# Where the expert-row pieces stand between the steps of two attention units, and two gate scalings one step earlier

## The chip, the cores and the metric

The kernel runs on one NeuronCore of a Trainium2 chip. TensorE (PE) multiplies matrices into PSUM, VectorE (DVE) and ScalarE (ACT) do the elementwise work, GpSimd (POOL) issues the indirect loads of expert rows, SyncE (SP) issues the weight loads. Each engine works through its own instructions in program order and waits on semaphores. The metric is the device time of one execution in microseconds (us); here the median of three executions.

## The reference

Two networks run one after the other on 256 tokens of width 1024, all in fp32. The first has two layers of attention, each followed by an expert layer:

```python
x = x + merged @ w_out[layer]
x = x + peer_ffn(rms_norm(x, norm2_g[layer]), w_query[layer], ...)
# peer_ffn, per token: 8 heads x 16 experts chosen by two top-k stages
act = gelu(einsum('td,ted->te', tb, expert_u[eb]))
out = einsum('te,ted->td', gb * act, expert_v[eb])
```

The second network, also of two layers, puts 16 meta tokens in front. A layer has a softmax mixer of 4 heads (MLA), a retention mixer of 4 heads with a gate `rg` that passes through silu, an output projection, and a gated FFN of width 2816.

## The kernel before

**First network.** Its 256 tokens make four expert units (2 token tiles x 2 layers, numbered 0 to 3). An expert unit has 128 rows per token. Row number n of all tokens is one indirect load (`row<-in_experts,idx`): 128 partitions x 2048 fp32, the u half and the v half of the chosen expert. DVE multiplies the u half with the token and sums it (line 1972, a *dot*), ACT applies gelu to four dots at once (line 1464), and the v half is added to `acc` with its weight (line 1955, an *acc*).

**Second network.** It has four units too (`layer2(v)`): units 0 and 1 are the two layers for meta tokens plus the first 128 tokens (144 columns), units 2 and 3 the same for the last 128 tokens. The body of each engine's `layer2` is a generator. The code between two `yield`s is a *step*; PE, ACT and DVE have the same 42 steps. On DVE: steps 0 to 5 norm, query and key parts; 6 and 7 rotate `rq`; 8 and 9 scale the keys and rotate `rk`; 10 to 15 softmax, value and decay work, head by head; 16 to 18 the output norms, which end with `yT` (lines 2282, 2291, 2293); 19 and 20 the residual add; 21 and 22 the second norm; 23 to 41 the FFN.

**What runs side by side.** Units 0 and 1 of the second network run together with the rows of expert unit 3. `last_order()` writes one list for all engines: a step of the unit, or one *piece* of row work (`"rows"`). There are 248 pieces (31 groups of 8). `SHARE2[s]` says how many of them, in proportion, stand in front of step s. A group of four rows is eight pieces on DVE:

- pieces 1 and 2 of a group: a dot of this group and an acc of the group before
- pieces 3 and 4: a dot each
- pieces 5 and 6: an acc each (in piece 5 of every eighth group also the gates of the next part)
- piece 7: the four weights (line 1989), after ACT's gelu
- piece 8: nothing, or in four of eight groups a part of the choice of the next experts: `best_keys`, `best_pairs`, `best_experts` twice

In this part PE has no work for the rows. ACT does the gelu in piece 5, once DVE has done the dot of piece 4; its other work waits behind it. POOL loads a row into the place of one ten rows earlier, when the acc of that one is done, so the order of the pieces on DVE also sets when row loads start. SP loads weight tiles of 2 MB into two places; the load of tile n+2 starts when PE has finished the last matmul of tile n (`layer2_taken`).

**The gate scaling.** `gate_scaled(p)` (line 2161) waits until PE has filled `rgA` or `rgB` and multiplies it with the norm factor. PE makes `rgA` at the end of its step 11 and `rgB` at the end of its step 13 (line 956, after the matmuls of `turn`, `values` and `ret_sums`). ACT takes the result through tanh (line 1522, `silu_gate(0)` in step 12, `silu_gate(1)` in step 14), and DVE finishes it in `gated` (line 2166, steps 12 and 14).

Of the kernel before, what the change touches and what calls it, by code (L numbers as in the profile page):

```python
# [241 lines left out]
def first_columns(b, start, stop, n):  # L242
# [2 lines left out]


TURN = 8
SHARE2 = ([0.6, 1.8, 0.8, 0.8, 0.9, 0.4, 0.9, 0.6, 0.8, 1.2, 1.6, 1.6, 1.6, 1.8, 1.6, 1.0, 2.0, 1.0, 1.0, 2.2, 1.6, 2.4, 0.0]
          + [1.4] + [2.1] * (FC // 2 - 1) + [1.4] * KC)
STEPS2 = len(SHARE2)  # L250


def last_order():

    beside = [0] * STEPS2 + [1] * (STEPS2 - KC)
    share = SHARE2 + SHARE2[:STEPS2 - KC]
    pieces = (PAIRS * GROUPS - 1) * TURN
# [16 lines left out]
def program(nc, x_in, meta_in, ws, c1_in, c2_in, fin_g, rel, k1_in, k2_in, euv, out):  # L274
    with ExitStack() as ctx:
# [1402 lines left out]
        def _(dve):  # L1678
# [331 lines left out]
            def layer2(v):  # L2010
# [10 lines left out]
                def bstep(ins):  # L2021
                    ins.then_inc(b_step, 1)
                    settled["b"] += 1

                def bsettle():
                    dve.wait_ge(b_step, settled["b"])
# [55 lines left out]
                def centered(name, dst, m, k):  # L2082
                    U.filled(dve, name)
                    b = U.bank(name)[0:m, :].rearrange("p (h e) -> p h e", h=RH)
                    bstep(dve.tensor_reduce(stb[0:m, 130:134], b, AX.X, ALU.add))
                    bsettle()
                    square = stb[0:m, 170 + k - 1:171 + k - 1]
                    bstep(dve.tensor_scalar(stb[0:m, 134:138], stb[0:m, 130:134], square, -1.0 / P, ALU.mult, ALU.mult))
                    bsettle()
                    U.inc(stt(dst.rearrange("p (h e) -> p h e", h=RH), b, square,  # L2090
                              stb[0:m, 134:138].unsqueeze(2).to_broadcast([m, RH, P]), ALU.mult, ALU.add), "b_rv")

                def s_read(name):
                    i = U.s_use(name)
                    U.wait(dve, "b_s", i + 1)
                    return S[(BASE["b_s"][v] + i) % 2]
# [20 lines left out]
                def decayed(h):  # L2117
                    b = s_read(f"r{h}")
                    if h >= 2:
                        U.wait(dve, "b_o", O_USES.index(f"r{h - 2}") + 1)  # L2120
                    d = k2st[:, K2_D + T2 * h:K2_D + T2 * (h + 1)]
                    if t:
                        tt_(rp[0:META, h % 2, 0:P], b[0:META, 0:P], d[0:META, T0:T2], ALU.mult)
                        m = tt_(rp[:, h % 2, P:3 * P], b[:, P:3 * P], d[:, 0:2 * P], ALU.mult)
                    else:
                        tt_(rp[0:META, h % 2, 0:T0], b[0:META, 0:T0], d[0:META, 0:T0], ALU.mult)
                        m = tt_(rp[:, h % 2, T0:T0 + P], b[:, T0:T0 + P], d[:, 0:P], ALU.mult)
                    U.inc(m, "b_sr")
# [28 lines left out]
                def gate_scaled(p):  # L2157
                    name = f"rg{'AB'[p]}"
                    U.filled(dve, name)
                    U.wait(dve, "b_rr", 4)  # L2160
                    U.inc(tt_((rot1 if t else rot0)[:, :, 0:T], two(U.bank(name)), each(bcs[:, 0:T], 2), ALU.mult), "b_rg")
# [95 lines left out]
                probs(1)  # L2257
                if not t:
                    centered("rvm", rvm[l][:], META, 2)
                yield  # L2260
                gate_scaled(0)
                logits(3)
                probs(2)
                decayed(0)
# [1 line left out]
                yield  # L2266
                probs(3)
                decayed(1)
                yield
                gate_scaled(1)  # L2270
                decayed(2)
                gated(1)
                yield
# [86 lines left out]
            for _ in window_order(1, attend, experts, layer2):  # L2360
                pass
# [174 lines left out]
```

## Time and profile before

| | |
|---|---|
| median of three executions | 2486.65 us (2485.22 to 2486.80) |
| the profiled execution, its own time | 2485.22 us |
| its span, first to last instruction | 2483.4 us |
| busy: PE, DVE, POOL, ACT | 2165.2, 1576.9, 632.3, 457.4 us |
| mean granted TensorE clock | 0.935 |
| mean DMA rate | 363 GB/s |

Busy shares are means over stages that differ. The stages of interest lie between 1419 and 2058 us: unit 0 up to the FFN (1419 to 1548), FFN of unit 0 (to 1752), unit 1 up to its FFN (to 1869), FFN of unit 1 (to 2058). In a line of the timeline the number in brackets is the idle time of the engine just ahead and what ended it; "issue" there means that the profile shows no releaser.

### The profile page before, as it was taken

To read this page: it belongs to the slowest core of one execution; us is meant where nothing else is said; L and a number is where in the kernel's file an instruction comes from. 1 tells how busy PE (TensorE), PEld (TensorE's weight loads), DVE (VectorE), ACT (ScalarE), POOL (GpSimd) and SP (SyncE) were. 2 spreads that over 40 slices of the span, in tenths; PEclk is the share of its full clock that TensorE was granted. 3 is DMA by queue.
4 is the path that set the end of the run, shared out by engine and by line. 5 is a ranking of instruction groups with operands and counts; after the bars stand their busy time and mean duration, and the time that the engine had idled before them with its cause. 6 is when DMAs were issued, how large, how long until landed. Compare 5 with 4: busy or idle time off the path is not lost.

```text
span 2483.4 us, 40088 instructions
## 1 busy us (share of the span) xinstructions
PE 2165.2 (87%) x16356; PEld 2006.1 (81%) x16356; DVE 1576.9 (63%) x4201; ACT 457.4 (18%) x984; POOL 632.3 (25%) x518
## 2 busy tenths in 40 slices
PE   9998899777889978688986788887887799999999
PEld 7887689777779868677986776877867798899799
DVE  1258688686777868869777689885788533312310
ACT  2210232101123011113301132100231012101100
POOL 0023334333334333334333223332133200000000
PEclk9999899989989979899998898989989899999999
DMA  8589999999999999999999977999979969468474
GB/s 330 186 372 422 421 421 418 422 421 419 422 414 417 422 411 421 418 423 411 392 421 418 420 310 312 415 422 403 371 293 403 423 227 387 174 242 314 167 256 154
DMA packets 106917, 900.95 MB, mean 363 GB/s; under 512 B 12748, under 2 KB 16880, under 8 KB 17904
## 3 DMA queue, kind: packets, MB, share of 16 engines
q0 software_dynamic: 73904, 537.43, 52.9%
q1 hardware_dynamic: 31728, 357.95, 36.4%
q8 instruction: 130, 2.13, 0.3%
q10 hardware_dynamic: 1104, 3.02, 0.3%
q14 instruction: 51, 0.42, 0.0%
HBM read 897.30 MB, written 1.05 MB: 362 GB/s over the span
## 4 chain that ended last, share of the span: by engine, by line
PE 39%; DMA 36%; DVE 18%; issue 4%; POOL 2%; ACT 1%; SPq 0%; DVEq 0%; POOLq 0%; ACTq 0%
DMA row<-in_experts,idx 20%; PE ea L956 11%; PE pa L956 10%; DMA more<-in_experts,idx 8%; DMA wring<-in_weights 8%; DVE row L1972 5%; DVE acc L1955 3%; PE ea L874 2%; PE pa L676 2%; PE pa L782 2%; POOL row L2388 1%; DVE topi L1864 1%; PE pa L829 1%; PE ea L964 1%; DVE topv L1860 1%
## 5 line engine op out<-in xcount | busy, mean ns | idle before, releaser
L2388 POOL DMA_INDIRECT row<-in_experts,idx x448 | 556.8, 1243 | 1198.7 <-DVE acc L1955 559.1
L1972 DVE CUSTOM_DVE_ANT_0 row<-row,h2n 128x1024 f32<-128x1024 f32 x448 | 534.9, 1221 | 187.4 <-DMA row<-in_experts,idx 186.5
L874 PE MATMUL ea<-diag,row 128*128 128x128 f32 x3808 | 497.7, 296 | 139.1 <-DVE diag L1994 139.1
L874 PEld LDWEIGHTS ea<-diag,row 128*128 128x128 f32 x3808 | 486.3, 211 | 152.1 <-DVE diag L1994 150.6
L1955 DVE SCALAR_TENSOR_TENSOR acc<-row,wgt,acc 128x1024 f32<-128x1024 f32 x207 | 265.1, 1281 | 2.0
L1464 ACT ACTIVATE gl<-dots 128x4 f32<-128x4 f32 x128 | 26.3, 206 | 945.1 <-DVE dots L1972 945.0
L956 PE MATMUL ea<-hB,wring 128*128 128x144 f32 (+1 forms) x1056 | 147.7, 304 | 20.9 <-DMA wring<-in_weights 20.9
L956 PEld LDWEIGHTS ea<-hB,wring 128*128 128x128 f32 x1056 | 144.0, 208 | 23.3 <-DMA wring<-in_weights 22.8
L956 PE MATMUL pa<-hB,wring 128*128 128x144 f32 (+1 forms) x1056 | 137.6, 291 | 17.6 <-DMA wring<-in_weights 15.0
L956 PEld LDWEIGHTS pa<-hB,wring 128*128 128x128 f32 x1056 | 133.9, 197 | 21.0 <-DMA wring<-in_weights 16.2
L782 PE MATMUL pa<-hA,wring 128*128 128x128 f32 x960 | 123.1, 281 | 0.0
L782 PEld LDWEIGHTS pa<-hA,wring 128*128 128x128 f32 x960 | 111.7, 191 | 14.0 <-issue 10.6
L1972 DVE CUSTOM_DVE_ANT_0 more<-more,h2n 128x1024 f32<-128x1024 f32 x64 | 77.3, 1224 | 50.8 <-DMA more<-in_experts,idx 50.8
L2388 POOL DMA_INDIRECT more<-in_experts,idx x64 | 73.8, 1153 | 120.2 <-DVE acc L1955 97.9
L676 PE MATMUL pa<-hA,wring 128*128 128x128 f32 x768 | 87.8, 275 | 0.5 <-DMA wring<-in_weights 0.5
L676 PEld LDWEIGHTS pa<-hA,wring 128*128 128x128 f32 x768 | 86.9, 192 | 1.2 <-DMA wring<-in_weights 0.7
L1464 ACT ACT_TABLE_LOAD x63 | 80.8, 1283 | 1.1
L956 PE MATMUL ea<-hB,wlate 128*128 128x128 f32 x672 | 77.4, 275 | 1.2 <-DVE hB L2045 1.2
L956 PEld LDWEIGHTS ea<-hB,wlate 128*128 128x128 f32 x672 | 76.3, 192 | 1.5 <-issue 1.5
L956 PE MATMUL ea<-actT,wring 128*128 128x144 f32 (+1 forms) x484 | 63.9, 296 | 11.8 <-DMA wring<-in_weights 11.8
L956 PEld LDWEIGHTS ea<-actT,wring 128*128 128x128 f32 x484 | 62.6, 201 | 12.6 <-DMA wring<-in_weights 12.6
L956 PE MATMUL pa<-actT,wring 128*128 128x144 f32 (+1 forms) x484 | 61.4, 288 | 5.9 <-DMA wring<-in_weights 5.8
(540 smaller groups left out, 3245.6 us busy)
## 6 DMA issues: line engine op xcount, KB each, us to landing
wring<-in_weights SPq DMA_DIRECT2D x110, 2048.0 KB, 12.0
wlate<-in_weights SPq DMA_DIRECT2D x25, 2048.0 KB, 8.3
wring<-in_weights SPq DMA_DIRECT2D x22, 1408.0 KB, 6.8
wlate<-in_weights SPq DMA_DIRECT2D x10, 1408.0 KB, 6.5
more<-in_weights SPq DMA_DIRECT2D x5, 2048.0 KB, 8.1
row<-in_experts,idx POOLq DMA_INDIRECT x448, 19.0
row<-in_weights SPq DMA_DIRECT2D x3, 2048.0 KB, 16.6
wring<-in_weights SPq DMA_DIRECT2D x3, 1792.0 KB, 11.1
```

The source lines that it names most:

```text
L676: m = pe.matmul(b[:, c * P:(c + 1) * P], w[:, k, (c0 + c) * P:(c0 + c + 1) * P], act[:, k, :], start=k == 0, stop=k == kcs - 1)
L782: m = pe.matmul(b[:, (i % 4) * P:(i % 4 + 1) * P], w[:, k, (i % 4) * P:(i % 4 + 1) * P], hA[:, k, :], start=k == 0, stop=k == KC - 1)
L829: m = pe.matmul(b[:, c * P:(c + 1) * P], w[:, k, c * P:(c + 1) * P], raw[:, k, :], start=k == 0, stop=k == KC - 1)
L874: m = pe.matmul(EA[c // 4][:, (c % 4) * P:(c % 4 + 1) * P], v[:, c * P:(c + 1) * P], diag[:, DIAG_SLOTS * (q % 2) + i, :], start=False, st ...
L956: x = pe.matmul(b[0:m, i * T:(i + 1) * T], w[:, k, c:c + m], act[:, k, 0:T], start=k == 0, stop=k == kcs - 1)
L964: x = pe.matmul(b[0:m, :], act[:, k, r], w[:, k, c:c + 512], start=k == 0, stop=k == kcs - 1)
L1464: act.activation(gl[:, g % 2, :], dots[:, g % 2, :], ACT.Gelu).then_inc(gelu_done, 1)
L1860: m = dve.max(v[:, 8 * a:8 * a + 8], x)
L1864: m = dve.max_index(q[:, 8 * a:8 * a + 8], v[:, 8 * a:8 * a + 8], x)
L1955: m = stt(acc[:], v, w, acc[:], ALU.mult, ALU.add)
L1972: dve.tensor_tensor_reduce(out=r, in0=r, in1=h2n[:, u % 2, :], scale=1.0, scalar=0.0, op0=ALU.mult, op1=ALU.add, accum_out=dots[:, g % 2, ...
L2388: pool.indirect_dma_start(out=expert_rows[slot], out_offset=None, in_=table, in_offset=bass.IndirectOffsetOnAxis(ap=idx[:, k % 2, GB * g + ...
```

## The change

Two things change. The list `SHARE2` gets other numbers for steps 5 to 8, 12, 14, 16 and 19 to 22:

```diff
-SHARE2 = ([0.6, 1.8, 0.8, 0.8, 0.9, 0.4, 0.9, 0.6, 0.8, 1.2, 1.6, 1.6, 1.6, 1.8, 1.6, 1.0, 2.0, 1.0, 1.0, 2.2, 1.6, 2.4, 0.0]
+SHARE2 = ([0.6, 1.8, 0.8, 0.8, 0.9, 0.8, 1.8, 1.8, 1.6, 1.2, 1.6, 1.6, 1.0, 1.8, 1.0, 1.0, 1.0, 1.0, 1.0, 1.6, 1.6, 0.9, 0.6]
           + [1.4] + [2.1] * (FC // 2 - 1) + [1.4] * KC)
```

And on DVE both gate scalings move to the end of the step before:

```diff
                     centered("rvm", rvm[l][:], META, 2)
-                yield
                 gate_scaled(0)
+                yield
                 logits(3)
...
                 decayed(1)
-                yield
                 gate_scaled(1)
+                yield
                 decayed(2)
```

In numbers of pieces done ahead of a step (counted from the start of unit 0; worked out from `last_order`):

| ahead of step | 5 | 6 | 7 | 8 | 9 | 10 | 11 | 12 | 13 | 14 | 15 | 16 | 17 | 18 | 19 | 20 | 21 | 22 |
|---|---|---|---|---|---|---|---|---|---|---|---|---|---|---|---|---|---|---|
| unit 0 before | 12 | 14 | 15 | 17 | 19 | 23 | 26 | 30 | 34 | 38 | 40 | 44 | 46 | 49 | 53 | 57 | 62 | 62 |
| unit 0 after | 13 | 17 | 21 | 24 | 27 | 30 | 34 | 36 | 40 | 42 | 45 | 47 | 49 | 51 | 55 | 58 | 60 | 62 |
| unit 1 before | 149 | 150 | 151 | 153 | 156 | 159 | 163 | 166 | 170 | 174 | 176 | 180 | 183 | 185 | 190 | 193 | 199 | 199 |
| unit 1 after | 149 | 153 | 157 | 161 | 163 | 167 | 170 | 173 | 177 | 179 | 181 | 183 | 186 | 188 | 191 | 195 | 197 | 198 |

Also, piece 144 (`best_keys`) stands ahead of step 3 of unit 1 before, and ahead of step 2 after. In the FFN steps the two programs differ by at most one piece. In units 2 and 3 nothing stands between the steps, so there the order of every engine stays as it was. The PE program is the same throughout.

On DVE, unit 0, from the end of step 5 on (qr is the rotated query, rq the retention query): before, two accs and then the rotation of `rq`, and one weight piece ahead of step 7 (line 2219).

```order
L2068 TENSOR_TENSOR soft<-qr,k2st 32x288
L2071 TENSOR_TENSOR qr<-qr,k2st 128x288
L2073 TENSOR_TENSOR qr<-qr,soft 128x288
L1955 SCALAR_TENSOR_TENSOR acc<-row,wgt,acc 128x1024 x2
L2055 TENSOR_TENSOR h2n<-ea,k2st 64x288
L2056 TENSOR_TENSOR h2n<-ea,k2st 64x288
L2058 TENSOR_TENSOR rq<-ea,k2st 128x288
L2060 TENSOR_TENSOR rq<-rq,h2n 128x288
L1989 TENSOR_TENSOR wgt<-gl,gates 128x4
L2219 RECIPROCAL stb<-stb 128x8
```

After, in the same place:

```order
L2073 TENSOR_TENSOR qr<-qr,soft 128x288
L1955 SCALAR_TENSOR_TENSOR acc<-row,wgt,acc 128x1024
L1989 TENSOR_TENSOR wgt<-gl,gates 128x4
L1860 MAX topv<-keys 128x8 x4
L1864 MAX_INDEX topi<-topv,keys 128x8 x4
L1869 MATCH_REPLACE keys<-topv,keys 128x128 x4
L1860 MAX topv<-keys 128x8 x4
L1864 MAX_INDEX topi<-topv,keys 128x8 x4
L1972 ISA row,dots<-row,h2n 128x1024
L1972 ISA dots 128x1
L1955 SCALAR_TENSOR_TENSOR acc<-row,wgt,acc 128x1024
L2055 TENSOR_TENSOR h2n<-ea,k2st 64x288
```

`best_keys` (lines 1860 to 1869) and a dot now stand ahead of the rotation; four more pieces (17 to 21) follow it ahead of line 2219.

On DVE, unit 0, from the end of `decayed(1)` (step 13) to `gated(1)`; line 2161 is `gate_scaled(1)`. Before:

```order
L2127 TENSOR_TENSOR soft<-s,k2st 128x128
L1972 ISA row,dots<-row,h2n 128x1024
L1972 ISA dots 128x1
L1972 ISA row,dots<-row,h2n 128x1024
L1972 ISA dots 128x1
L1955 SCALAR_TENSOR_TENSOR acc<-row,wgt,acc 128x1024 x2
L2161 TENSOR_TENSOR h2n<-ea,bcs 128x288
L2126 TENSOR_TENSOR soft<-s,k2st 16x144
L2127 TENSOR_TENSOR soft<-s,k2st 128x128
L2166 SCALAR_TENSOR_TENSOR h2n<-h2n 128x288
```

After:

```order
L2126 TENSOR_TENSOR soft<-s,k2st 16x144
L2127 TENSOR_TENSOR soft<-s,k2st 128x128
L2161 TENSOR_TENSOR h2n<-ea,bcs 128x288
L1972 ISA row,dots<-row,h2n 128x1024
L1972 ISA dots 128x1
L1955 SCALAR_TENSOR_TENSOR acc<-row,wgt,acc 128x1024
L1972 ISA row,dots<-row,h2n 128x1024
L1972 ISA dots 128x1
L1955 SCALAR_TENSOR_TENSOR acc<-row,wgt,acc 128x1024
L2126 TENSOR_TENSOR soft<-s,k2st 16x144
L2127 TENSOR_TENSOR soft<-s,k2st 128x128
L2166 SCALAR_TENSOR_TENSOR h2n<-h2n 128x288
```

The scaling now follows `decayed(1)` at once, with no row work between; two pieces instead of four come behind it.

On DVE, unit 0, from `decayed(3)` (step 15) to line 2277 (step 16), which takes the sums of `sm`. Before:

```order
L2127 TENSOR_TENSOR soft<-s,k2st 128x128
L1972 ISA row,dots<-row,h2n 128x1024
L1972 ISA dots 128x1
L1955 SCALAR_TENSOR_TENSOR acc<-row,wgt,acc 128x1024
L1972 ISA row,dots<-row,h2n 128x1024
L1972 ISA dots 128x1
L1955 SCALAR_TENSOR_TENSOR acc<-row,wgt,acc 128x1024
L1972 ISA row,dots<-row,h2n 128x1024
L1972 ISA dots 128x1
L1972 ISA row,dots<-row,h2n 128x1024
L1972 ISA dots 128x1
L2277 RECIPROCAL stb<-stb 128x8
```

After:

```order
L2126 TENSOR_TENSOR soft<-s,k2st 16x144
L2127 TENSOR_TENSOR soft<-s,k2st 128x128
L1955 SCALAR_TENSOR_TENSOR acc<-row,wgt,acc 128x1024
L1989 TENSOR_TENSOR wgt<-gl,gates 128x4
L2277 RECIPROCAL stb<-stb 128x8
```

Four dots and two accs less stand between the two.

## Rows read from the trace of the kernel before

**Rows 1.** Windows, four stages: length, busy time of each engine, PEclk, DMA share, GB/s.

```profile
1419.00:1548.00 129.00, 110.11 (x642) 88.68 (x643) 112.12 (x298) 44.20 (x97) 36.51 (x25) 0.85 0.80 315
1548.00:1752.00 204.00, 164.87 (x1212) 161.27 (x1211) 145.14 (x299) 17.15 (x39) 58.24 (x44) 0.92 1.00 414
1752.00:1869.00 117.00, 101.69 (x592) 79.53 (x592) 104.81 (x273) 40.09 (x82) 37.06 (x25) 0.88 0.83 323
1869.00:2058.00 189.00, 163.05 (x1219) 160.39 (x1219) 104.56 (x185) 18.45 (x47) 34.23 (x25) 0.94 0.90 354
```

**Rows 2.** Chain of waits, FFN of unit 0: start, us, what.

```profile
1587.20 10.51 DMA wring<-in_weights
```

**Rows 3.** Waits of DVE, 1419 to 1548 (unit 0): us, times, longest.

```profile
DVE h2n L2055 <- PE ea L956: 2.4, 1, 2.4
DVE h2n L2055 <- PE pa L1181: 1.7, 1, 1.7
DVE stb L2085 <- PE ea L964: 1.4, 1, 1.4
DVE stb L2285 <- ACT stb L1639: 1.4, 1, 1.4
DVE stb L2219 <- ACT stb L1484: 0.8, 1, 0.8
```

**Rows 4.** Waits of DVE, 1752 to 1869 (unit 1).

```profile
DVE kpg L2199 <- ACT sqp L1481: 3.8, 1, 3.8
DVE stb L2085 <- PE ea L964: 2.5, 1, 2.5
DVE soft L2126 <- issue: 1.7, 1, 1.7
DVE h2n L2055 <- PE ea L956: 0.6, 1, 0.6
```

**Rows 5.** Timeline of DVE, unit 0: dot, acc, dot; `best_keys` and the dot behind it.

```profile
1430.03 1.22 DVE L1972 CUSTOM_DVE_ANT_0 row<-row,h2n 128x1024 f32<-128x1024 f32 x1
...
1431.17 1.28 DVE L1955 SCALAR_TENSOR_TENSOR acc<-row,wgt,acc 128x1024 f32<-128x1024 f32 x1
1432.37 1.22 DVE L1972 CUSTOM_DVE_ANT_0 row<-row,h2n 128x1024 f32<-128x1024 f32 x1
...
1462.71 0.87 DVE L1860 MAX8 topv<-keys 128x8 f32<-128x128 f32 x4
...
1468.05 1.22 DVE L1972 CUSTOM_DVE_ANT_0 row<-row,h2n 128x1024 f32<-128x1024 f32 x1
```

**Rows 6.** Timeline of DVE, unit 0: `best_experts` and the dot behind it.

```profile
1510.04 0.17 DVE L1905 CAST bestf<-bestp 128x16 f32<-128x16 uint32 x1
...
1513.98 1.22 DVE L1972 CUSTOM_DVE_ANT_0 row<-row,h2n 128x1024 f32<-128x1024 f32 x1
```

**Rows 7.** Timeline of PE, unit 0: `turn(2)` and `turn(3)`; `rgB` lies between.

```profile
1509.01 0.69 PE L1022 MATMUL ptb<-kst,soft 128*128 128x128 f32 x2 [3.84 <-DVE soft L2115]
...
1520.07 0.38 PE L1022 MATMUL ptb<-kst,soft 128*128 128x128 f32 x2
```

**Rows 8.** Timeline of PE, unit 1: the same two.

```profile
1834.08 0.69 PE L1022 MATMUL ptb<-kst,soft 128*128 128x128 f32 x2 [3.26 <-DVE soft L2115]
...
1844.74 0.38 PE L1022 MATMUL ptb<-kst,soft 128*128 128x128 f32 x2
```

**Rows 9.** Timeline of DVE, unit 0: first dot behind `decayed(3)`, then step 16.

```profile
1530.23 1.20 DVE L1972 CUSTOM_DVE_ANT_0 row<-row,h2n 128x1024 f32<-128x1024 f32 x1
...
1537.19 0.19 DVE L2277 RECIPROCAL stb<-stb 128x8 f32<-128x8 f32 x1
```

**Rows 10.** Timeline of ACT, unit 0: table load and square root ahead of step 16.

```profile
1532.26 1.28 ACT L1632 ACT_TABLE_LOAD   x1
1535.26 0.27 ACT L1632 ACTIVATE stb<-ea,eps 128x8 f32<-128x8 f32 x1 [1.72 <-PE ea L1073]
```

**Rows 11.** Timeline of PE, unit 1: start of `g0` in the FFN.

```profile
1889.84 5.86 PE L956 MATMUL pa<-soft,wring 128*128 128x144 f32 x32 [4.72 <-DMA wring<-in_weights]
```

More of the change, by code:

```diff
@@ L2259, in layer2 @@
                     centered("rvm", rvm[l][:], META, 2)
+                gate_scaled(0)
                 yield
-                gate_scaled(0)
                 logits(3)
@@ L2268, in layer2 @@
                 decayed(1)
+                gate_scaled(1)
                 yield
-                gate_scaled(1)
                 decayed(2)
```

## The prediction

> **What bounds the kernel now.** I read the page first, then the windows by stage, then the chain of waits, then the waits and the timeline of DVE in the two places that change. The page's busy shares (PE 87%, DVE 63%) say little, because they mix stages. The windows [rows 1] separate them. In the two stretches where the softmax and retention steps of units 0 and 1 run beside the row pieces, DVE is busy 112.12 of 129 us and 104.81 of 117 us, while the DMA engines are busy 0.80 and 0.83 of the time. In the FFN stretches behind them it is the other way round: DMA share 1.00 and 0.90, and in the chain PE waits 10.51 us for a weight tile [rows 2], a step that repeats with every tile of the FFN of unit 0. So each unit has a part in which DVE sets the pace and PE and DVE hand work to each other, and a part in which the bytes set it. The change reorders DVE in the first part and leaves the bytes alone. It takes nothing away and adds nothing: 62 pieces stand ahead of step 22 of unit 0 in both programs, 61 or 60 of their own in unit 1. What it can alter is how long DVE stands idle there, and that is small: in unit 0 the waits between step 6 and step 18 are 2.4 + 1.7 + 1.4 + 1.4 + 0.8 = 7.7 us [rows 3], in unit 1 from step 2 on they are 3.8 + 2.5 + 1.7 + 0.6 = 8.6 us [rows 4]. These are the most that any order could win. Waits of 0.4 us for a square root within step 7 are there in both orders and left out.
>
> **Prices of pieces.** A dot takes 1.14 us and an acc 1.20 us from start to start; `best_keys` takes 1468.05 - 1462.71 = 5.34 us [rows 5], `best_experts` 1513.98 - 1510.04 = 3.94 us [rows 6]. The weight piece is about 0.2 us.
>
> **Steps 5 to 9: pieces moved forward.** Unit 0 has 8 pieces more ahead of step 9 (27, not 19). They hold the holes shut in which DVE waited for `sqk` (0.8), for `rqB` (1.7) and for `rkB` (2.4): 4.9 us gone [rows 3]. PE still gets its inputs later, since pieces 16 to 21 (5.34 + 2 x 2.34 + 2 x 1.14 + 1.20 = 13.5 us) now stand ahead of step 7 and so of its key roots; but DVE had as much work in front, so nothing is lost yet. What comes in its place is on ACT. The gelu of piece 21 now stands directly ahead of ACT's square roots for step 7; it needs the dot of piece 20, and then comes a table load of 1.28 us [rows 10] and about 0.7 us of activations, while DVE has one acc (1.20) left. I count 0.9 us of waiting, between 0 (the table load gets out of the way) and 2.
>
> The Trainium skill (ScalarE: Activation LUTs, What ACT_TABLE_LOAD costs) puts every switch of tables at about 2.66 us, a load of 1283 ns and a drain of 1380 ns. The trace shows the load of 1.28 us, but no drain: in rows 10 the idle time that is counted behind it (1.72 us, waiting for PE) begins when the load ends. By the page the wait would be 2.3 us per unit and the sum below 2.8 us larger; I go by the trace.
>
> **Unit 1, step 2.** `best_keys` now runs ahead of `kpg`, which DVE waited 3.8 us for [rows 4]. It takes 5.34 us, so the hole closes completely and `kpg` comes 1.6 us later, with no one waiting for it yet (PE's `qr` follows after two more groups). 3.8 us gone. The 0.6 us for `rkB` may become anything from 0 to 1.9, because PE gets the keys later; I take 1.0.
>
> **Step 10, `rv`.** DVE waits for PE's `rv` (1.4 and 2.5 us). In the new order PE starts `rv` when `meta_probs` is done, and DVE has 3 and 4 pieces meanwhile: 0.9 and 1.4 us by my count.
>
> **Steps 11 and 12, `gate_scaled(0)`.** While PE makes `rvm` and `rgA`, DVE has the pieces ahead of step 11 (in both units `best_experts`, two dots and two accs: 3.94 + 2 x 2.34 = 8.6 us) and then step 11 itself. I cost the move at nothing; with that cover gone it would cost what I take below for `rgB` without its `best_experts`, 4.8 us per unit.
>
> **Step 13, `gate_scaled(1)`: a new wait.** From `turn(2)`, which follows `probs(2)` at once, to `turn(3)`, which starts right behind `rgB`, PE needs 1520.07 - 1509.01 = 11.06 us in unit 0 [rows 7] and 1844.74 - 1834.08 = 10.66 us in unit 1 [rows 8]. Before, four pieces of step 13 and four of step 14 stood between. Now `gate_scaled(1)` follows `decayed(1)`. In unit 0 DVE has `decayed(0)` and `gated(0)` (an estimate of 1.1, short instructions like those in rows 9), pieces 37 to 40 (2 x 1.20 + 0.2 + 3.94 = 6.5) and step 13 (again 1.1): 8.7 us, so it waits 2.3 us. In unit 1 pieces 174 to 177 hold no `best_experts` (1.20 + 0.2 + 2.34 = 3.7): 5.9 us, so it waits 4.8 us. Bounds: 0 if `rgB` is done early, 6 if PE runs at its lower clock throughout. Behind the waiting instruction stand two pieces and `decayed(2)`, and behind that PE's `ret_sums(2)`. ACT's `silu_gate(1)` gets its input earlier, but nothing on the path waits for it.
>
> **Step 16, the norm sums: a new wait.** After `decayed(3)` PE does `ret_sums(3)` and `sm`, then ACT the square root, done at 1535.26 + 0.27 [rows 10]; `decayed(3)` ended at 1530.23 [rows 9]. That is 5.3 us. Before, four pieces, with accs 6.96 us long, covered it, and line 2277 ran at 1537.19 with no idle time. Now an acc and a weight piece are left: 1.4 us. DVE waits 3.9 us in each unit. The wait of 1.4 us behind it, for `sr`, stays in unit 0.
>
> **The sum.** Unit 0: before 7.7; after 0.9 + 0.9 + 2.3 + 3.9 + 1.4 = 9.4; +1.7 us. Unit 1: before 8.6; after 0.9 + 1.0 + 1.4 + 4.8 + 3.9 = 12.0; +3.4 us. Together +5.1 us.
>
> Does it reach the end? `yT` becomes ready later by this and by the pieces that now stand ahead of step 18 (2 more in unit 0, 3 more in unit 1, about 3.5 and 4.6 us of DVE). These pieces are then missing in the FFN stretch, where a row costs its load: 537.43 MB / 512 = 1.05 MB at 414 GB/s [rows 1] is 2.5 us. One row less in each FFN, 2.5 us, against one row more, 2.3 us of DVE, in front: an even trade, and I let the idle time pass through to the end. Against the profiled execution's own 2485.22 us that is 2490.3; the median of before lies 1.4 us above this execution, so the forecast is 2491.8 us.
>
> **Rivals.** *The early pieces win (faster).* The holes of rows 3 and 4 close, 4.9 us in unit 0 and 3.8 + 0.6 in unit 1, and the new waits fall where DVE does not end the stage: in unit 1 PE waited 4.72 us for a tile at `g0` anyway [rows 11]. For it speaks also that DMA is idle 20% of the 129 us [rows 1], and row loads that start 3 to 4 rows earlier use this. It decides from the point where the entry of the FFN waits on a load and not on `yT`. 2486.65 - 9.3 = 2477.4 us. Against it: the tile of `g0` is asked for only when PE has finished `outB`, which needs `yT`. Chance 0.21.
>
> *No change.* The orders meet again: ahead of step 22 both have done 62 pieces, and with 2 pieces instead of 5 ahead of step 21 the root comes earlier behind `outD`. By this count unit 0 starts its FFN tiles at the same time, and if the bytes alone set the rest, 2486.7 us, give or take 3. Against it: later tile requests leave DMA idle in a stretch in which it was full. Chance 0.28.
>
> *The exit does not give back (slower by more).* A later `yT` delays the requests of the next tiles, while fewer rows stand ready to use the DMA in the meantime, so the 3.5 and 4.6 us are not returned: 5.1 + 8.1 = 13.2, 2499.9 us. For it: the chain through the FFN is made of tile loads [rows 2]. Chance 0.16.
>
> My forecast holds the other 0.35.
>
> **How the numbers follow.** A measurement of this kernel tells about 0.2% (5 us) from no change. The forecast of +5.1 lies on this border; I give 0.13 of its 0.35 to "same" and 0.22 to "slower". With the third rival and a little of the second that makes slower 0.42; same 0.36; faster 0.22. The waits that the trace lets vanish bound the time below: no more than 7.7 + 8.6 us; half of this is where the first rival ends. The range is 2478 to 2500 us; the forecast alone would be 2487 to 2497.
>
> **What would show it.** Right: a wait of DVE line 2161 for PE of 2 us in unit 0 and near 5 in unit 1; a wait of line 2277 for ACT line 1632 near 4 us in both; no wait of line 2199 in unit 1 and none of the first `rkB` rotation in unit 0; `yT` later by 5 us or more, and the FFN stretches shorter by one row each. Wrong: line 2161 without a wait (PE was ahead), or DVE waiting for row loads in steps 5 to 9, which I count at nothing because the load of a row starts at the acc ten rows ahead, and so at least five dots before its own; or an FFN of unit 0 that begins its tile loads earlier than before.

## The result, and the profile after

The changed kernel takes 2499.30 us (median of 6, 2495.09 to 2504.79) against 2485.94 us (2484.54 to 2489.94) for the kernel before beside it: 13.4 us slower, ratio 1.0058 [1.0044, 1.0073]. The forecast was 2491.8 us: right in direction, too small by more than half. The profiled execution took 2504.26 us, so it lies 5 us above its median. Its span of 2502.5 us is 19.1 us longer than that of before, not 13.4; the seven stretches in the table below make 18.1 us of this.

Windows of the changed kernel, the same four stages as in [rows 1]; length, busy time of PE, PE loads, DVE, ACT, POOL, PEclk, DMA share, GB/s:

```profile
1419.00:1554.00 135.00, 108.20 (x642) 87.35 (x642) 116.13 (x306) 40.27 (x95) 37.14 (x26) 0.87 0.82 319
1554.00:1763.50 209.50, 169.94 (x1213) 167.17 (x1212) 141.56 (x294) 16.06 (x39) 57.77 (x43) 0.89 0.96 391
1763.50:1890.00 126.50, 105.60 (x592) 84.76 (x592) 108.94 (x280) 35.94 (x80) 32.80 (x26) 0.84 0.86 329
1890.00:2077.50 187.50, 164.06 (x1224) 161.80 (x1224) 100.33 (x178) 18.12 (x46) 30.87 (x24) 0.93 0.86 338
```

Both fronts are longer (129 to 135, 117 to 126.5). The FFN of unit 0, which was to become shorter, went from 204 to 209.5 us; its DMA share fell from 1.00 to 0.96 and its clock from 0.92 to 0.89.

Waits of DVE, changed kernel, unit 0 (answers to [rows 3]):

```profile
DVE stb L2277 <- ACT stb L1632: 4.8, 1, 4.8
...
DVE h2n L2161 <- PE ea L956: 1.9, 1, 1.9
DVE h2n L2055 <- PE pa L956: 1.0, 1, 1.0
DVE stb L2085 <- PE ea L964: 1.0, 1, 1.0
DVE stb L2219 <- ACT stb L1484: 0.9, 1, 0.9
```

The same, unit 1 (answers to [rows 4]):

```profile
DVE h2n L2161 <- PE ea L956: 5.7, 1, 5.7
DVE stb L2277 <- ACT stb L1632: 4.9, 1, 4.9
DVE stb L2085 <- PE ea L964: 1.4, 1, 1.4
DVE h2n L2055 <- PE ea L956: 0.9, 1, 0.9
DVE stb L2219 <- ACT stb L1484: 0.9, 1, 0.9
```

The wait of line 2199 (3.8 us) is gone, and so is the 2.4 us of line 2055. The two new waits stand where they were forecast. With 0.2 us left of the wait for `sr` in unit 0 they come to 4.8 + 1.9 + 1.0 + 1.0 + 0.9 + 0.2 = 9.8 us in unit 0 and 5.7 + 4.9 + 1.4 + 0.9 + 0.9 = 13.8 us in unit 1, against 7.7 and 8.6 before: +7.3 us, forecast +5.1. A wait of 0.5 us of line 2166 for ACT in unit 1 is new too and not in this sum.

One execution does not settle this size. In a second profiled execution of the changed kernel the same waits come to 14.4 us in unit 0 and 13.4 in unit 1, +11.5 us. Three of those of unit 0:

```profile
DVE stb L2085 <- PE ea L964: 3.7, 1, 3.7
DVE h2n L2161 <- PE ea L956: 3.1, 1, 3.1
DVE h2n L2055 <- PE pa L956: 1.7, 1, 1.7
```

Of the loss that was not forecast the larger part lies behind `yT` in the first execution, and about half in the second. The table gives the stretches of one profiled execution each, from starts in the timeline of DVE: *front* from line 2199 (`kpg`) to the first line 2291 (`yT`), *exit* from there to line 2317, *FFN* to the last line 2342. "idle" is the idle time of the DMA engines, summed from windows of 2.5 us.

| kernel | front 0 | exit 0 | FFN 0 | between | front 1 | exit 1 | FFN 1 | idle, exit 0 + FFN 0 |
|---|---|---|---|---|---|---|---|---|
| before | 105.5 | 33.1 | 170.5 | 15.2 | 102.6 | 34.8 | 157.3 | 0.4 + 2.6 |
| before, again | 105.5 | 33.1 | 170.5 | 15.2 | 102.7 | 34.7 | 157.5 | 0.3 + 2.6 |
| after | 110.7 | 31.6 | 177.2 | 16.8 | 110.8 | 34.0 | 155.9 | 6.4 + 7.1 |
| after, again | 115.3 | 31.3 | 174.9 | 16.9 | 110.4 | 30.1 | 157.8 | 6.2 + 4.3 |
| e3, late pieces early | 108.9 | 32.9 | 173.5 | 15.1 | 108.5 | 30.2 | 157.8 | 1.1 + 5.4 |
| d3, early half alone | 110.1 | 34.6 | 171.7 | 19.1 | 108.3 | 37.0 | 156.2 | 0.5 + 4.9 |
| d1, delay alone | 109.4 | 37.6 | 169.2 | 15.1 | 106.6 | 34.4 | 154.9 | 4.3 + 3.1 |
| d4, pieces later | 102.0 | 32.8 | 178.0 | 14.0 | 101.8 | 36.6 | 156.7 | 2.4 + 3.2 |
| e6, unit 0 alone | 112.2 | 33.4 | 176.0 | 15.7 | 104.4 | 35.2 | 156.4 | 8.7 + 5.7 |

After: the fronts with the stretch between the units (where `best_keys` now stands, ahead of line 2199) are 5.2 + 1.6 + 8.2 = 15.0 us longer. Exit and FFN of unit 0 add 5.2 us more instead of giving 3.5 back; those of unit 1 give back 2.2 us instead of 4.6. The sum is 18.0. Against the forecast (13.2 us ahead of the two `yT`, 8.1 us back behind them) the first execution is off by 1.8 us ahead and 11.1 behind. The second has 19.3 us ahead and gives back 1.6 behind, so it is off by 6.1 and 6.5.

Where the DMA engines stood idle shows in the first 10 us behind `yT`. Kernel before, unit 0 and unit 1:

```profile
1544.93:1554.93 10.00, 8.68 (x64) 8.04 (x65) 9.79 (x22) 0.91 (x4) 3.54 (x3) 1.00 0.99 396
...
1866.36:1876.36 10.00, 8.68 (x50) 8.04 (x51) 9.72 (x21) 0.20 (x1) 2.61 (x2) 0.83 1.01 419
```

The changed kernel, the same stretches:

```profile
1551.11:1561.11 10.00, 8.84 (x53) 8.24 (x54) 7.31 (x18) 0.65 (x2) 3.72 (x3) 0.83 0.54 175
...
1887.57:1897.57 10.00, 8.71 (x65) 8.04 (x65) 7.38 (x22) 0.88 (x3) 2.33 (x2) 1.00 0.55 195
```

PE is busy with the output projection, its next tile can't be requested, and only rows could fill the DMA engines. Before, rows requested late fill them (share 0.99, 1.01). After, those rows had been requested and loaded ahead of `yT`, where 36.2 MB moved instead of 32.9 in unit 0, and the share is 0.54 and 0.55. The whole exit of unit 0, before and (second line) after:

```profile
1544.93:1578.04 33.11, 26.81 (x194) 25.52 (x194) 25.32 (x53) 4.55 (x12) 10.95 (x8) 0.95 1.00 408
1551.11:1582.70 31.59, 26.46 (x194) 25.40 (x194) 21.92 (x49) 5.56 (x11) 7.30 (x6) 0.95 0.81 311
```

That is 13.5 MB before and 9.8 after. In the FFN of unit 0 it is 70.8 and 71.0 MB (windows below). The rows loaded ahead are missing in the exit, not in the FFN where the forecast had taken one out.

The chain of waits of the changed kernel then shows what follows:

```profile
1561.70 10.14 DMA wring<-in_weights
```

The tile of `g0`, the first product of the FFN, is requested when PE has finished `outB`, the second quarter of the output projection, at 1561.70. PE, before and (second fence) after:

```profile
1566.02 5.76 PE L956 MATMUL pa<-soft,wring 128*128 128x144 f32 x32 [4.00 <-DMA wring<-in_weights]
```

```profile
1571.89 4.19 PE L956 MATMUL pa<-soft,wring 128*128 128x144 f32 x32 [2.38 <-DMA wring<-in_weights]
```

PE starts `g0` 5.9 us later for a `yT` that is 6.2 us later. The request alone is 7.5 us later (it was at 1554.21); the load takes 10.1 us instead of 11.8 and makes most of the difference good. In the FFN of unit 0 PE waits about as long for tiles as before, but in fewer and longer waits. Waits of PE there (total, times, longest), before and (second fence) after:

```profile
PE pa L956 <- DMA wring<-in_weights: 18.1, 6, 5.1
PE ea L956 <- DMA wring<-in_weights: 15.0, 6, 6.0
```

```profile
PE pa L956 <- DMA wring<-in_weights: 26.1, 6, 6.1
PE ea L956 <- DMA wring<-in_weights: 8.5, 4, 4.5
```

Behind the long waits here PE is slower. PE, changed kernel:

```profile
1607.27 6.14 PE L956 MATMUL pa<-hB,wring 128*128 128x144 f32 x32 [6.11 <-DMA wring<-in_weights]
1613.25 8.00 PE L956 MATMUL ea<-hB,wring 128*128 128x144 f32 x64
...
1630.22 6.60 PE L956 MATMUL pa<-hB,wring 128*128 128x144 f32 x32 [5.05 <-DMA wring<-in_weights]
```

Before, behind a short wait:

```profile
1608.32 4.19 PE L956 MATMUL ea<-hB,wring 128*128 128x144 f32 x32 [2.45 <-DMA wring<-in_weights]
```

32 matmuls take 4.2 us behind a wait of 2.45 us and 6.1 to 6.6 us behind waits of 5 to 6 us. The wait alone does not decide it: at 1619.03 in the kernel before such a group takes 5.86 us behind 2.60 us. PE starts a slow group (over 5 us) 6 times in the FFN of unit 0 before and 8 times after, 5 and 8 times in the second executions. The FFN of unit 0 as a whole, before and (second fence) after:

```profile
1578.04:1748.53 170.49, 136.37 (x995) 133.60 (x996) 119.27 (x249) 12.35 (x28) 48.08 (x36) 0.92 1.00 415
```

```profile
1582.70:1759.92 177.22, 141.75 (x995) 139.63 (x996) 118.81 (x249) 9.96 (x26) 51.11 (x38) 0.87 0.97 401
```

PE is busy 5.4 us longer with the same 995 matmuls, at a granted clock of 0.87 instead of 0.92. The next tile waits for PE, so the slower PE is also idle time of the DMA engines.

### The profile page after: what moved, and what is told of

It is laid out like the page before. It is cut to its first block, busy times and chain, and to the rows that moved or that the text cites. A ratio compares the mean times of both kernels' runs of the same rounds, so it can differ in the third digit from the quotient of the medians.

```text
span 2502.5 us, 40080 instructions
## 1 busy us (share of the span) xinstructions
PE 2172.3 (87%) x16356; PEld 2015.8 (81%) x16356; DVE 1575.6 (63%) x4201; ACT 447.7 (18%) x977; POOL 628.6 (25%) x518
## 3 DMA queue, kind: packets, MB, share of 16 engines
q1 hardware_dynamic: 31728, 357.95, 36.2%
HBM read 897.30 MB, written 1.05 MB: 359 GB/s over the span
## 4 chain that ended last, share of the span: by engine, by line
PE 41%; DMA 33%; DVE 18%; issue 4%; POOL 2%; ACT 1%; another core or an unknown queue 0%; DVEq 0%; POOLq 0%; ACTq 0%
DMA row<-in_experts,idx 18%; PE pa L956 11%; PE ea L956 10%; DMA more<-in_experts,idx 8%; DMA wring<-in_weights 7%; DVE row L1972 5%; PE ea L874 3%; DVE acc L1955 3%; PE pa L676 3%; PE pa L782 2%; POOL row L2388 1%; DVE topi L1864 1%; PE ea L964 1%; DVE more L1972 1%; PE pa L684 1%
## 5 line engine op out<-in xcount | busy, mean ns | idle before, releaser
L2388 POOL DMA_INDIRECT row<-in_experts,idx x448 | 551.1, 1230 | 1243.8 <-DVE acc L1955 592.0
L956 PE MATMUL pa<-hB,wring 128*128 128x144 f32 (+1 forms) x1056 | 155.2, 313 | 38.7 <-DMA wring<-in_weights 34.9
L956 PEld LDWEIGHTS pa<-hB,wring 128*128 128x128 f32 x1056 | 151.3, 217 | 42.5 <-DMA wring<-in_weights 36.6
L956 PE MATMUL ea<-hB,wring 128*128 128x144 f32 (+1 forms) x1056 | 136.7, 292 | 1.3 <-DMA wring<-in_weights 1.3
L956 PEld LDWEIGHTS ea<-hB,wring 128*128 128x128 f32 x1056 | 134.7, 198 | 1.8 <-DMA wring<-in_weights 1.5
L956 PEld LDWEIGHTS ea<-actT,wring 128*128 128x128 f32 x484 | 62.4, 201 | 10.4 <-DMA wring<-in_weights 10.4
```

The lines of the kernel that those rows point to most:

```text
L956: x = pe.matmul(b[0:m, i * T:(i + 1) * T], w[:, k, c:c + m], act[:, k, 0:T], start=k == 0, stop=k == kcs - 1)
L2388: pool.indirect_dma_start(out=expert_rows[slot], out_offset=None, in_=table, in_offset=bass.IndirectOffsetOnAxis(ap=idx[:, k % 2, GB * g + ...
```

## Experiments

Each ratio is against the kernel before on the same chip. 0.2% is 5 us. In most kernels a table overrides the count of pieces ahead of single steps:

```diff
-        while done < round(at / sum(share) * pieces):
+        while done < AHEAD.get((v, s - v * STEPS2), round(at / sum(share) * pieces)):
```

**e1_share, e2_gates: the two parts of the change apart.** In e1 the gate scalings stand as before, in e2 the list does.

```diff
 # e1_share, against the changed kernel; gate_scaled(1) likewise
-                gate_scaled(0)
                 yield
+                gate_scaled(0)
```

> The new numbers of SHARE2 alone; both gate scalings stand where they stood before. Theory W (the time follows the waits of DVE ahead of yT, and what comes later trades evenly): the wait of line 2161 goes in unit 0 (1.9 us in the changed kernel) and falls from 5.7 to about 2.2 us in unit 1, since two pieces (3.5 us) cover it; the waits of line 2277 stay near 4.8 us. That is 5.4 us below the changed kernel (2499.3): about 2494. Theory X (a later yT also delays the requests of the next weight tiles, and this costs more than the waits): yT comes earlier by the same 5.4 us, and what the exit costs stays, so the time is also about 2494, but the FFN of unit 0 is still some us longer than before. Rival G (the gate move is what costs, through ACT and PE): within 2 us of before, 2486 to 2488.

> Only the two gate scalings move one step earlier; the pieces stand as before. In the trace of before rgB is filled at 1520.1 us and decayed(1) ends at 1519.6 in unit 0, in unit 1 at 1844.7 and 1844.7: the new waits would be 0.7 and 0.3 us, and rgA is filled ahead of its step. Theories W and X: +1 us at most, 2486 to 2487. Rival G: most of the 13.4 us, 2496 or more.

Measured: e1 2498.65 us, 1.0042 [1.0027, 1.0058]; e2 2491.45 us, 1.0016 [1.0005, 1.0026]. The list makes most of the loss. Both expectations were missed. e2 lies above the 2487 of theories W and X and far below G: the gates cost about 4 us, though their two new waits are only 0.81 and 0.51 us; their FFN of unit 0 is 2.2 us longer at a clock of 0.90. e1 lies above the 2494 of W and X: line 2161 waits less, as expected, but other waits take the place (line 2285 1.9 us instead of 0.2 in unit 0; lines 2126, 2199 and 2166 1.7, 1.4 and 1.0 us in unit 1), and the fronts, 110.6 and 109.3 us, are hardly shorter than with the gates moved. In e1 line 2161 waits not at all in unit 0 and 2.3 us in unit 1, so of the 7.6 us that it waits in the changed kernel the two parts together are needed.

**e3_exit_early: only the late counts,** moved ahead of step 18.

```diff
+AHEAD = {(0, 18): 51, (0, 19): 55, (0, 20): 58, (1, 18): 188, (1, 19): 191, (1, 20): 195}
```

> Before, with two more pieces ahead of step 18 of unit 0 and three more ahead of step 18 of unit 1 (and so fewer in steps 19 to 21), as in the changed kernel; nothing else. DVE gets no new wait ahead of yT, but yT comes 3.5 and 4.6 us later. Theory W: an even trade, 2486 (up to +2). Theory X: the later yT delays outB and with it the next tile requests, +5 to +8 us: 2491 to 2494.

Measured: 2494.01 us, 1.0024 [1.0013, 1.0035], +6.0 us. That is theory X's size. `yT` comes 3.4 and 5.9 us later (fronts). One wait is new, 1.2 us in unit 1:

```profile
DVE stb L2285 <- ACT stb L1639: 1.2, 1, 1.2
```

Unit 0 gives nothing back (exit and FFN 2.8 us longer), unit 1 4.6 us in its exit. An even trade would have been 0. The first 10 us behind `yT` of unit 0, and PE in that exit:

```profile
1549.38:1559.38 10.00, 9.19 (x46) 8.65 (x47) 7.36 (x18) 0.65 (x2) 3.69 (x3) 0.66 0.96 378
```

```profile
1550.19 6.70 PE L956 MATMUL pa<-yT,wring 128*128 128x144 f32 x24 [4.54 <-DVE yT L2293]
...
1571.36 4.19 PE L956 MATMUL pa<-soft,wring 128*128 128x144 f32 x32 [2.70 <-DMA wring<-in_weights]
```

The DMA engines are not idle here (share 0.96, 1.1 us in the whole exit), and still `g0` starts 5.3 us later than before for a `yT` that is 4.5 us later. So it does not take idle DMA engines behind `yT` to pass a later `yT` on. In unit 1 `g0` starts 10.1 us later for a `yT` 13.1 us later.

**e4_exit_late: the changed kernel with the late counts of before.**

```diff
+AHEAD = {(0, 17): 47, (0, 18): 49, (0, 19): 53, (0, 20): 57, (0, 21): 62, (1, 17): 183, (1, 18): 185, ...}
```

> The changed kernel up to step 16, and from step 17 on the piece counts of before (49, 53, 57, 62 ahead of steps 18 to 21 of unit 0; 185, 190, 193, 199 in unit 1). yT comes 3.5 and 4.6 us earlier than in the changed kernel; the waits of DVE ahead of it stay. Theory W: no change from 2499.3 (within 2 us). Theory X: 5 to 8 us less, 2491 to 2494.

Measured: 2503.81 us, 1.0067 [1.0053, 1.0081]. Both theories were missed: taking pieces away ahead of `yT` brought it forward by 1.0 and 0.4 us only (fronts 109.7 and 110.4), because waits took their place. In unit 1 (waits of DVE):

```profile
DVE h2n L2161 <- PE ea L956: 5.4, 1, 5.4
DVE stb L2277 <- ACT stb L1632: 4.9, 1, 4.9
DVE stb L2285 <- ACT stb L1639: 2.8, 1, 2.8
DVE yT L2282 <- PE pa L946: 1.5, 2, 1.3
```

The last two are not in the changed kernel. Its late pieces were the cover of waits that its early pieces had made. The first 10 us behind `yT` of unit 0:

```profile
1550.60:1560.60 10.00, 8.69 (x50) 8.04 (x51) 9.34 (x20) 1.04 (x3) 3.55 (x3) 0.83 0.52 174
```

With as many pieces ahead of step 18 as before, the DMA engines are as idle as in the changed kernel. So the idle exit comes with the early order of the pieces, and the late ones alone do not make it (e3).

**d3_front: only the early counts,** back to those of before by step 14.

```diff
+AHEAD = {(0, 5): 13, (0, 6): 17, (0, 7): 21, (0, 8): 24, (0, 9): 27, (0, 10): 30, (0, 11): 33, (0, 12): 35, (0, 13): 37, ...}
```

> The early half of the change alone: the counts of the changed kernel in steps 5 to 10 of both units (and best_keys ahead of step 2 of unit 1), brought back to those of before by step 14, so that the covers of lines 2161, 2277 and 2285 and all of the exit stay as before; gate scalings as before. If the holes of steps 2 to 9 are worth what they measure (4.9 us in unit 0, 3.8 + 0.6 in unit 1) less 0.9 for the square roots of step 7, yT comes 3 to 4 us earlier per unit and the time is 2479 to 2483 us. If DMA decides (the rows are requested earlier but the same number is in flight and the weight tiles of the front are requested when PE asks for them), or if PE merely reaches the same waits later, it is 2485 to 2489 us. Slower than 2490 would say that early pieces delay PE's chain through the keys by more than they fill.

Measured: 2500.04 us, 1.0042 [1.0029, 1.0056]. None of the ranges below 2490 held: moving pieces up to steps 5 to 9, and so out of steps 10 to 13, is by itself a loss as large as that of the whole list. With as many pieces ahead of `yT` as before, the fronts are 4.6 and 5.7 us longer. Waits of DVE in unit 1:

```profile
DVE stb L2085 <- PE pa L964: 3.7, 1, 3.7
DVE stb L2085 <- PE ea L964: 2.3, 1, 2.3
DVE kpg L2199 <- ACT sqp L1481: 2.2, 1, 2.2
```

And line 2161 in unit 0:

```profile
1527.45 0.46 DVE L2161 TENSOR_TENSOR h2n<-ea,bcs 128x288 f32<-128x288 f32 x1 [5.56 <-PE ea L956]
```

Two things meet in it. The pieces made PE's inputs late: `turn(0)` of unit 0, before and (second line) in d3, starts 10.9 us later, 9.7 of them counted from line 2199.

```profile
1489.99 0.38 PE L1022 MATMUL ptb<-kst,soft 128*128 128x128 f32 x2
1500.87 0.38 PE L1022 MATMUL ptb<-kst,soft 128*128 128x128 f32 x2
```

And the cover of line 2161 did not stay, as the expectation had it: between step 12 and step 14, 3 pieces stand in unit 0 instead of 8, and 5 instead of 8 in unit 1. The holes came back, larger, as waits for PE. How much each of the two makes is not parted.

**e5_cover16: the changed kernel with two pieces of cover moved from step 15 into the hole ahead of line 2277.** `AHEAD = {(0, 15): 43, (1, 15): 179}`.

> The changed kernel with two pieces moved from ahead of step 15 to ahead of step 16 in both units (43 and 47, 179 and 183). A dot and an acc more (2.35 us) cover the chain through sm: the wait of line 2277 falls from 4.8 to 2.4 us in each unit. Theory W+D: yT 2.4 us earlier per unit and about 4.7 us less in all, if a wait ahead of yT reaches the end at its full length: 2494 to 2495. Rival (the wait of line 2277 falls into time that the exit waits for anyway): within 1 us of the changed kernel.

Measured: 2499.11 us, 1.0045 [1.0031, 1.0059], against 1.0054 [1.0038, 1.0070] for the changed kernel run again in the same set (and 0.9999 [0.9989, 1.0008] for the kernel before run again). The intervals overlap: not told apart, and neither 2494 to 2495 nor the rival is shown. In its trace the wait of line 2277 falls to 1.4 and 2.6 us, and the fronts are 107.5 and 109.5 us.

**c1_holes: the kernel before with single pieces put into its holes.** `AHEAD = {(0, 7): 16, (0, 9): 20, (1, 2): 144, (1, 10): 160, (1, 15): 177, (1, 16): 181}`.

> The kernel before with single pieces put into its own holes: best_keys (piece 16) ahead of step 7 and piece 20 ahead of step 9 in unit 0; best_keys (144) ahead of step 2, piece 160 (best_experts) ahead of step 10, piece 177 ahead of step 15 and 181 ahead of step 16 in unit 1. All other counts as before. Theory W+D: the waits 0.8 + 1.7 and part of 2.4 us in unit 0 and 3.8 + 2.5 + 1.7 us in unit 1 close, at most 1 us of new waits arises, and up to 9 us are won, of which I expect 4 to 8: 2480 to 2484. Rival P (earlier pieces cost more than the holes they fill, because later ones lose their cover or DMA runs dry): not faster than before.

Measured: 2487.53 us, 1.0000 [0.9991, 1.0008]. A miss: filling the holes one by one gained nothing. In its trace, of an execution 9.6 us above the median, the fronts are 105.3 and 100.8 us and the stretch between the units is 4.4 us longer. Waits have moved: line 2055 waits 3.2 us for PE in unit 0, line 2285 waits 2.3 and 2.6 us for ACT.

**d1_delay: DVE kept busy ahead of `yT`, no piece moved.**

```diff
-                yield
+                yield; [(bstep(dve.tensor_reduce(stb[:, 162:163], kst[:, 0:562], AX.X, ALU.add)), bsettle()) for _ in range(5 if v < 2 else 0)]
```

> The kernel before, with idle-like work put on DVE directly ahead of the last products of yT (between line 2285 and line 2291) in units 0 and 1: five sums over 562 columns into an unused place, about 0.7 to 0.8 us each, some 4 us per unit; no piece is moved and no row is requested at another count. Theory A (the exit hands the delay on: the tile of g0 is requested only when PE has finished outC, and nothing behind it makes the time good): +4 us per unit, 2494 to 2496 us. Theory B (bytes decide: the rows requested up to then go on loading during the delay, and from yT to the end of the FFN of unit 0 only the bytes left and the idle time of the DMA engines count): the DMA engines work through the delay, so it is returned by more than half; 2487 to 2491 us. In the trace A has the stretch from yT to the first operation of the FFN as long as before (33 us) and the FFN of unit 0 too (170.5); B has one of them shorter by 2 us or more.

Measured: 2498.08 us, 1.0045 [1.0030, 1.0059], +7 to +15 us for a delay of 3.85 us per unit:

```profile
1546.55 3.82 DVE L2286 TENSOR_REDUCE stb<-kst 128x1 f32<-128x562 f32 x5
```

Theory A's 8 us are reached and probably passed; over both units nothing is returned. `g0` of unit 0 starts at 1571.73, 5.7 us later than before for a `yT` 5.5 us later. The exit of unit 0 is even 4.5 us longer (its FFN 1.3 us shorter), which A did not have. (The expectation lets the request wait for `outC`; the kernel waits for `outB`, as the prediction has it.) Windows of the exit of unit 0, d1:

```profile
1550.40:1588.00 37.60, 30.21 (x194) 29.04 (x194) 25.42 (x52) 4.37 (x11) 10.03 (x7) 0.82 0.90 359
```

Within it the first 10 us have a DMA share of 0.70, though no row was moved. PE, which waited 5.0 us for `yT`, does its 194 matmuls in 30.21 us at a clock of 0.82; before, the same 194 take 26.81 us at 0.95.

**d2_fewer: in unit 0, 44 pieces instead of 49 ahead of step 18, and 18 instead of 13 between step 18 and step 22.** `AHEAD = {(0, 14): 36, (0, 15): 38, (0, 16): 41, (0, 17): 42, (0, 18): 44, (0, 19): 48, (0, 20): 54, (0, 21): 60, ...}`.

> The mirror of the changed kernel's exit: the kernel before with pieces moved behind yT, 44 instead of 49 ahead of step 18 in unit 0 and 183 instead of 185 in unit 1, the covers of lines 2161 and 2277 kept at 2.3 and 6 us or more. yT comes 4.9 us earlier in unit 0 and 2.3 us or more earlier in unit 1. Theory A (what counts is when yT is ready, since the tile of g0 is requested from there): 5 to 7 us faster, 2480 to 2482 us. Theory B (before, the DMA engines have no idle time from yT to the end of the FFN of unit 0, 0.4 + 2.6 us, so rows that are moved there cost their load of 2.5 us each): 2.5 rows x 2.5 us = 6 us given back in unit 0, so no gain, 2485 to 2491 us, with the stretch behind yT or the FFN of unit 0 longer by about what yT gains.

Measured: 2493.32 us, 1.0022 [1.0013, 1.0032], above both theories. `yT` came 4.7 us earlier in unit 0 and the exit took 39.5 instead of 33.1 us, since PE now waited for DVE in it:

```profile
PE ea L925 <- DVE hB L2307: 6.1, 1, 6.1
```

That was my choice of places and no test of the trade, so d4 repeats it with an exit as before.

**d4_later: 46 pieces instead of 49 ahead of step 18, 13 in the exit, three more in the FFN** (182 instead of 185 in unit 1). `AHEAD = {(0, 14): 36, (0, 15): 38, (0, 16): 41, (0, 17): 43, (0, 18): 46, (0, 19): 50, ..., (0, 29): 92, ...}`.

> The trade of rows between the front and the FFN, in the other direction and with the exit unchanged: the kernel before with 46 instead of 49 pieces ahead of step 18 in unit 0 and 182 instead of 185 in unit 1, the same 13 or 14 pieces between step 18 and step 22, and the three pieces taken up over the FFN steps 23 to 29. The covers of lines 2161 and 2277 stay at 2.3 us and 6.5 (unit 0) or 4.9 us (unit 1). yT comes 2.5 us earlier per unit. Theory A (no trade: the time goes by when yT is ready, and the FFN takes a row more at no cost, as it gave nothing back for a row less): 5 to 6 us faster than before, 2481 to 2483 us. Theory B (even trade: a row more in the FFN costs its load, 2.5 us, because the DMA engines have no idle time from yT to the end of the FFN of unit 0): no change, 2485 to 2490 us, with yT earlier by 2.5 us and the stretch from yT to the end of the FFN of unit 0 (203.6 us) longer by 2 to 3. Theory C (any shift brings longer waits of PE for tiles and a lower granted clock in the FFN of unit 0): 2489 us or more, that stretch 206 us or more, and the granted clock of the FFN of unit 0 below 0.92.

Measured: 2490.07 us, 1.0008 [0.9998, 1.0019]. `yT` of unit 0 is 3.5 us earlier, the stretch behind it 7.2 us longer, with 85.1 MB moved in it instead of 84.3 and 5.6 us of idle DMA time instead of 3.0. FFN of unit 0 in d4:

```profile
1576.81:1754.81 178.00, 139.70 (x995) 137.58 (x996) 123.37 (x256) 10.80 (x28) 52.36 (x38) 0.89 1.00 411
```

A is out: nothing is won. B's time holds and its stretch does not: 7.2 us longer, not 2 to 3, for 0.8 MB more, which at 411 GB/s would be 2.0 us. All that C named is there: 2489 us or more, 210.8 us from `yT` to the end of the FFN, a granted clock of 0.89 instead of 0.92. So the run shows that three pieces more in the FFN bring no gain for an earlier `yT`. It does not show that a row there costs its load, since the lower clock and the idle time are in the same stretch. The profiled execution gets back 1.2 us between the units and 0.8 in the front of unit 1.

**e6_unit0: the changed counts in unit 0 alone,** gate scalings as before. The row of `U0` is that of the table of counts ahead of the prediction.

> The changed kernel's counts in unit 0 alone; unit 1 and both gate scalings as before. If the loss is the sum of the two units' later yT (5.2 us in unit 0 and 8.2 us in unit 1) handed on to the end, this costs 5 to 6 us: 2492 to 2494 us, with yT of unit 0 later by 4 to 5.5 us and unit 1 as before. If the loss sits in the FFN of unit 0 (longer by 4 to 7 us there, at a lower granted clock, beside the later yT), it is 9 to 11 us: 2496 to 2499 us. If unit 1 alone made it, 2486 to 2489 us.

Measured: 2497.37 us, 1.0031 [1.0021, 1.0041], +7.7 us by the ratio (5.2 to 10.2), the size expected for a loss in the FFN beside the later `yT`. About half of the loss or more comes from unit 0 (after: 5.2 - 1.5 + 6.7 = 10.4 of the 18.1 us of the profiled execution). The first 10 us behind its `yT`:

```profile
1553.93:1563.93 10.00, 8.85 (x54) 8.24 (x55) 7.31 (x18) 0.65 (x2) 3.69 (x3) 0.83 0.50 164
```

**How far `g0` follows `yT`.** Starts of line 2291 and of PE's first group for `g0`, against those of the kernel before, in us. "behind" is the time between the two, "share" that of DMA in the first 10 us.

| kernel | `yT`, unit 0 | `g0`, unit 0 | behind, unit 0 | share, unit 0 | behind, unit 1 |
|---|---|---|---|---|---|
| before | 0 | 0 | 21.1 | 0.99 | 23.5 |
| after | +6.2 | +5.9 | 20.8 | 0.54 | 21.5 |
| after, again | +11.1 | +10.4 | 20.5 | 0.52 | 20.5 |
| e3 | +4.5 | +5.3 | 22.0 | 0.96 | 20.5 |
| d1 | +5.5 | +5.7 | 21.3 | 0.70 | 20.9 |
| d3 | +5.8 | +6.6 | 21.9 | 0.99 | 20.4 |
| e4 | +5.7 | +6.8 | 22.2 | 0.52 | 20.6 |
| e6 | +9.0 | +8.9 | 21.0 | 0.50 | 23.9 |
| d4 | -1.0 | -1.5 | 20.6 | 0.79 | 20.5 |

In unit 0 a shift of `yT` is passed on to `g0` to within 1.1 us in these traces (1.5 to 2.1 us in e2, d2 and c1), whether the DMA engines are idle behind `yT` or not. In unit 1 it is passed on less 2 to 3 us in most of them.

## Why the prediction was wrong

- **The waits ahead of `yT`: right in place, short in size.** +7.3 us against +5.1 in the first profiled execution, +11.5 in the second. In the first, line 2161 waits 1.9 and 5.7 us (forecast 2.3 and 4.8), line 2277 4.8 and 4.9 us (3.9 each); line 2199 has no wait, the waits of line 2055 for `rqB` and `rkB` in unit 0 are gone, `rv` 1.0 and 1.4 (0.9 and 1.4). Line 2219 waits 0.9 us in both units, as forecast. The rotation of `rkB` costs 0.9 us in unit 1 (1.0), and that of `rkA`, a step earlier, 1.0 us in unit 0, which had not been counted. No DVE wait for a row falls into steps 5 to 9. The wait for `sr` shrank to 0.2 us instead of staying at 1.4; why is open, for in e1 it is 1.9 us behind the same wait of line 2277.
- **The pieces ahead of `yT`: right in size.** Forecast 3.5 and 4.6 us of DVE beside the waits of 1.7 and 3.4, 13.2 us in all; the two `yT` came 5.2 + 9.8 = 15.0 us later, and 7.3 us of that are waits (second execution: 19.3 and 11.5).
- **"One row less in each FFN, 2.5 us, against one row more, 2.3 us of DVE, in front: an even trade": this step failed.** The 8.1 us were not given back: behind the two `yT` the changed kernel is 3.0 us longer in one execution and 1.6 us shorter in the other. e3 moves exactly these late pieces and pays 6.0 us; d1 moves none, only makes `yT` late, and pays as well. The step priced a row in the FFN by the DMA share of 1.00 [rows 1], as if DMA time saved anywhere were time won. But what has to be done after `yT` is a chain: the output projection, the request for `g0`, its load. It starts when `yT` is ready: in unit 0 `g0` is shifted by as much as `yT` to within 1.1 us in the changed kernel, e3 and d1, in unit 1 by 2 to 3 us less. The row was not even missing where the step had it (unit 0): the FFN of unit 0 moved 71.0 MB instead of 70.8, the exit 9.8 instead of 13.5. Idle DMA engines in the exit go with this in the changed kernel (share 0.54), in e4 and in e6, but not in e3 and d3, so the loss does not need them; what they cost beside it is not shown. Nor does d4 show the price in the other direction, only that there is nothing to win there either.
- **A reading of [rows 2] was loose.** The 10.51 us are the load of a tile from request to landing. PE works on the tile before in most of this time and is idle for 1.42 and 1.05 us of it. The chain of tile loads was read rightly all the same.
- **The rival "the exit does not give back", 2499.9 us with a chance of 0.16, was the case.** Its first reason, later requests for the next tiles, is what the traces show. Its second, fewer rows ready to use the DMA engines, holds in the changed kernel and is not needed in e3. That its 13.2 us stand beside 13.4 is in part luck. It took 5.1 us of waits, where the two profiled executions have 7.3 and 11.5, and nothing given back, where they lose 3.0 more and give back 1.6. I had read the chain of tile loads [rows 2] and still gave it half the chance of the forecast.
- **The lower clock in the FFN of unit 0 was not forecast.** 5.4 us more of PE in the profiled execution. The second one has a clock of 0.89 and an FFN 4.4 us longer instead of 6.7. In e2, d3 and c1 a clock of 0.90 appears without a change of counts in the exit, so its share of the median's 13.4 us stays open; so does the part of e2's 4 us that its 1.3 us of waits do not explain.
- **"The early pieces win" fell** with c1 (no gain) and d3 (+7 to +14 us): where DVE waits in [rows 3] and [rows 4], PE or ACT sets the time, and work put there comes back as waits. The sum +5.1 counted such waits, but not all. The parts of the change do not add up: e3's 6.0, d3's 10.4 and e2's 4 us are more than 13.4, and e4 shows one reason, that the late pieces cover waits which the early ones make.

## What to carry to other kernels

A wait of the engine that hands over to a chain (DVE to PE and back) is not free room: work put there delays what the other engine gets, and the wait returns later, in d3 larger. When work is moved from behind a hand-over to ahead of it, first follow the chain that starts at the hand-over: if the next load is requested only along it, most of the delay is passed on. Then look where bytes loaded early will be missing; here it was the exit and not the FFN. A DMA share of 1.00 in a stage does not say that taking bytes away from it shortens it. And when parts of a change are tried alone, expect that they cover or uncover each other's waits.

## What the runs showed of the hardware

- Behind waits of 5 and 6 us PE runs 32 matmuls of 128x144 in 6.1 to 6.6 us instead of 4.2 (changed kernel, 1607.27 and 1630.22), and a granted clock of 0.82 stands over an exit with two waits of 4 and 5 us (d1). In a stage where each tile's request waits for PE, the slower group makes the next request later as well: in e3 the request for the tile of `g0` comes 6.6 us later for a `yT` 4.5 us later, behind a wait of PE of 4.54 us and 24 matmuls in 6.70 us.
- The kernel before repeats itself within 0.2 us in each of the seven stretches of two profiled executions (1 to 5 us had been expected behind `yT`). The changed one doesn't: its first front took 110.7 and 115.3 us. Outside these stretches traces differ too: line 2199 of unit 0 starts at 1439.46 us before and at 1441.92 in d4, whose order is the same up to there. So a difference of 1 or 2 us between two single traces carries no argument here.
